# SwiGLU up projections with weight blocks stationary and high and low activations in one moving operand

## The chip, the cores and the metric

One core of one Trainium2 chip runs the whole program. The metric is the device time of one launch in microseconds, as the median of the runs shown.

## What is computed

Two layers work on 256 tokens of width 1024. Each layer is a feed-forward block, a mixer (projections, dilated and neighbourhood attention, gates, output projection) and a second feed-forward block, and a norm closes the program. The change is in the feed-forward blocks, whose inner width is 2816:

```python
def swiglu(x, w_up, w_down):
    gate, up = jnp.split(x @ w_up, 2, axis=-1)
    return (jax.nn.silu(gate) * up) @ w_down

for l in range(DEPTH):
    x = x + 0.5 * swiglu(rms_norm(x, ffn1_norm[l]), ffn1_w_up[l], ffn1_w_down[l])
    x = x + hybrid_mixer(rms_norm(x, mix_norm[l]), ...)
    x = x + 0.5 * swiglu(rms_norm(x, ffn2_norm[l]), ffn2_w_up[l], ffn2_w_down[l])
return rms_norm(x, final_norm)
```

## The kernel before

All large products run in split float32: each operand is a high part (rounded to fp32r) and a low part (the rest), and one product is three matmuls, high x high, high x low and low x high (`product`, L1017 to L1019). ScalarE (ACT) makes the high part of each weight unit (`hi`, L522), VectorE (DVE) the low part (`lo`, L721).

Weights come in units of 1 MB through a ring of three slots (`raw`, `w_hi`, `w_lo`). A unit's DMA is issued when the unit three before it has its low part; its high part is made when TensorE (PE) has finished with the unit three before (`split_free`). One feed-forward block is 33 units: 11 chunks of 256 hidden columns with three units each, two for the up projection (gate and up columns side by side, four of the eight k-blocks of 128 per unit) and one for the down projection.

In the up projection the normalised input's transpose (`a_hi`, `a_lo`, 128x128 blocks) is stationary and 512 weight columns move: 2 token halves x 8 k-blocks x 3 = 48 matmuls of 512 columns per chunk. ACT takes the tanh of the gate half (`tanh`, L575), DVE makes the gated tile `hidden` from it (`hide`, L800 and L803). PE turns `hidden` with four 128x128 transposes (`turn`, L1103), ACT and DVE split the turned tile (`hT_upper` L582, `hT_lower` L810), and the down product (24 matmuls of 512 columns) adds to four banks of 512 output columns, the groups g0 to g3. A chunk's down product runs one chunk late: PE's loop is first half of up(c), turn(c-1), second half of up(c), down(c-1). Each engine's queue is in the written order.

Between two blocks PE finishes the last down unit group by group; DVE adds each group to `x` (`update`, L732), PE transposes `x` (`input_transposes`, L1055), ACT and DVE split the result (`transposed_hi` L530, `transposed_lo` L745), ACT sums squares for the norm (L540) and GpSimd (POOL) turns the sums into `rstd`. The next block's first unit is split by `next_hi` and `next_lo` before those steps. In the mixer's output projection (units O_AT to O_AT+3) the groups end in the same way. In the first block, PE runs matmuls on a zero tile (`spin`, L1048) while the input arrives.

## Time and profile before

| | us |
|---|---|
| median of 3 runs (lowest, highest) | 1189.36 (1189.19, 1190.08) |
| the profiled execution | 1190.11 |
| its span | 1188.3 |
| granted TensorE clock, mean | 0.998 |

Busy time in the span: PE 1174.7 us (99%), PE's weight loads 965.4 us (81%), DVE 717.5 us (60%), ACT 561.7 us (47%), POOL 59.6 us (5%). Of the 5632 matmuls, 4560 belong to split products of 512 columns. Matmuls overlap each other in the profile, so that the step from one start to the next is the pace, and not the duration of one.

### The profile page before, as it was taken

The numbers are of one execution on the slowest core, as the hardware profiler recorded it, in microseconds if no ns is written. First come the engines' busy times: TensorE is split into PE (matmuls) and PEld (weight loads), VectorE is DVE, ScalarE is ACT, GpSimd is POOL, SyncE is SP. The second block draws the span as 40 slices with busy tenths as digits, with TensorE's granted clock in tenths as the row PEclk, the third lists the DMA queues.
The fourth block names the chain that finished last, engine by engine and source line by source line (L and its number), as shares of the span: only waits on it lengthen the run. The fifth ranks groups of instructions, "written<-read, shape, count | busy, mean of one in ns | idle before, by whom it ended". The sixth has DMA issues, their size and how long they took to land.

```text
span 1188.3 us, 15620 instructions
## 1 busy us (share of the span) xinstructions
PE 1174.7 (99%) x5632; PEld 965.4 (81%) x5632; DVE 717.5 (60%) x992; ACT 561.7 (47%) x767; POOL 59.6 (5%) x70
## 2 busy tenths in 40 slices
PE   8999999999999999999999999999999999999997
PEld 5888888888888888888888888878888888888885
DVE  4555556756766665555575555577557566655555
ACT  6444445555534544444464444465554445444342
POOL 3300003000200000000000000200002000000000
PEclk9999999999999999999999999999999999999999
DMA  9966555653434465555545555655443435655551
GB/s 269 288 208 205 181 204 176 206 177 109 141 130 154 152 211 186 194 178 199 187 164 193 182 187 195 230 177 177 142 142 107 164 138 177 213 191 197 179 174 36
DMA packets 145594, 211.47 MB, mean 178 GB/s; under 512 B 7648, under 2 KB 112272, under 8 KB 145296
## 3 DMA queue, kind: packets, MB, share of 16 engines
q1 hardware_dynamic: 142960, 206.33, 51.8%
q0 software_dynamic: 1920, 3.20, 1.2%
q10 hardware_dynamic: 672, 1.37, 0.4%
q8 instruction: 28, 0.46, 0.2%
q14 instruction: 14, 0.11, 0.0%
HBM read 209.77 MB, written 4.19 MB: 180 GB/s over the span
## 4 chain that ended last, share of the span: by engine, by line
PE 90%; DVE 4%; ACT 3%; issue 2%; DMA 0%; ACTq 0%; POOLq 0%; POOL 0%; DVEq 0%
PE bank L1017 28%; PE bank L1019 27%; PE bank L1018 27%; PE bank L1200 2%; PE bank L1173 2%; PE bank L1103 2%; DVE w_lo L721 1%; PE bank L1185 1%; ACT w_hi L522 1%; ACT a_hi L530 1%; DVE a_lo L745 1%; PE bank L1163 1%; ACT probs L540 1%; PE bank L1055 1%; DVE qk_raw L924 0%
## 5 line engine op out<-in xcount | busy, mean ns | idle before, releaser
L721 DVE TENSOR_TENSOR w_lo<-raw,w_hi 128x2048 fp32r<-128x2048 f32 x190 | 440.0, 2318 | 243.3 <-ACT w_hi L522 243.2
L522 ACT ACTIVATE w_hi<-raw 128x2048 fp32r<-128x2048 f32 x190 | 363.7, 1918 | 252.4 <-PE bank L1019 238.3
L1017 PE MATMUL bank<-w_hi,a_hi 128*128 128x512 f32 (+1 forms) x1152 | 460.5, 400 | 1.5 <-DVE probsT L803 0.4
L1019 PE MATMUL bank<-w_hi,a_lo 128*128 128x512 f32 (+1 forms) x1152 | 446.7, 388 | 0.0
L1018 PE MATMUL bank<-w_lo,a_hi 128*128 128x512 f32 (+1 forms) x1152 | 445.7, 387 | 0.0
L1017 PEld LDWEIGHTS bank<-w_hi,a_hi 128*128 128x128 f32 x1152 | 216.7, 188 | 49.5 <-issue 5.8
L1019 PEld LDWEIGHTS bank<-w_hi,a_lo 128*128 128x128 f32 x1152 | 216.4, 188 | 45.5
L1018 PEld LDWEIGHTS bank<-w_lo,a_hi 128*128 128x128 f32 x1152 | 217.0, 188 | 39.0
L1017 PE MATMUL bank<-w_hi,hT_hi 128*128 128x512 f32 x352 | 138.2, 393 | 0.4 <-DVE hT_lo L810 0.4
L1019 PE MATMUL bank<-w_hi,hT_lo 128*128 128x512 f32 x352 | 137.1, 389 | 0.0
L1018 PE MATMUL bank<-w_lo,hT_hi 128*128 128x512 f32 x352 | 137.0, 389 | 0.0
L582 ACT ACTIVATE hT_hi<-bank 128x256 fp32r<-128x256 f32 x88 | 29.5, 383 | 153.1 <-PE bank L1103 153.1
L575 ACT ACTIVATE probs<-bank,stat 128x256 f32<-128x256 f32 x88 | 41.8, 475 | 123.5 <-PE bank L1019 123.5
L1017 PEld LDWEIGHTS bank<-w_hi,hT_hi 128*128 128x128 f32 x352 | 66.1, 188 | 14.1 <-DVE w_lo L721 0.9
L1019 PEld LDWEIGHTS bank<-w_hi,hT_lo 128*128 128x128 f32 x352 | 66.1, 188 | 13.9
L1018 PEld LDWEIGHTS bank<-w_lo,hT_hi 128*128 128x128 f32 x352 | 66.1, 188 | 13.3
L810 DVE TENSOR_TENSOR hT_lo<-bank,hT_hi 128x256 fp32r<-128x256 f32 x88 | 33.6, 420 | 70.4 <-ACT hT_hi L582 70.3
L800 DVE SCALAR_TENSOR_TENSOR probs<-probs,bank 128x256 f32<-128x256 f32 x88 | 36.8, 419 | 30.4 <-ACT probs L575 30.4
L845 DVE COPY probsT<-bank 128x512 f32<-128x512 f32 (+1 forms) x40 | 23.4, 585 | 45.2 <-PE bank L1185 45.2
L641 ACT ACTIVATE probs<-probs,neg_top 128x256 f32<-128x256 f32 (+1 forms) x80 | 36.6, 460 | 23.9 <-DVE neg_top L871 23.9
L803 DVE SCALAR_TENSOR_TENSOR probsT<-probs,stat,bank 128x256 f32<-128x256 f32 x88 | 42.3, 481 | 3.1
L1200 PEld LDWEIGHTS bank<-v,probsT 128*128 128x128 f32 x256 | 34.7, 191 | 3.3
(89 smaller groups left out, 655.6 us busy)
## 6 DMA issues: line engine op xcount, KB each, us to landing
raw<-ffn_w_up_dram SPq DMA_DIRECT2D x172, 512.0 KB, 4.5
raw<-w_in_dram SPq DMA_DIRECT2D x92, 512.0 KB, 4.4
raw<-ffn_w_down_dram SPq DMA_DIRECT2D x88, 512.0 KB, 3.9
raw<-w_out_dram SPq DMA_DIRECT2D x16, 512.0 KB, 3.6
raw<-w_branch_b_dram SPq DMA_DIRECT2D x8, 512.0 KB, 3.8
bias_rows<-na_rel_bias_dram POOLq DMA_DIRECT2D x24, 128.0 KB, 6.1
...
```

The source lines that it names most:

```text
L522: act.activation(w_hi[slot][:, :], raw[slot][:, :], ACT.Copy).then_inc(hi_done, 1)
L575: act.activation(tanh_g[:, t, :], bank[UP[t]][:, 0:FC], ACT.Tanh, scale=half_rstd[:, t:t + 1]).then_inc(tanh_done, 1)
L582: act.activation(hT_hi[:, :, toks], bank[HT[t]][:, 0:2 * P].rearrange("p (k s) -> p k s", k=2), ACT.Copy).then_inc(hT_hi_done, 1)
L641: e = act.activation(part, part, ACT.Exp, bias=neg_top[:, h, t:t + 1], accum_out=den[:, h, t:t + 1])
L721: dve.tensor_tensor(w_lo[slot][:, :], raw[slot][:, :], w_hi[slot][:, :].bitcast(F32), ALU.subtract).then_inc(lo_done, 1)
L800: dve.scalar_tensor_tensor(gated[:, t, :], tanh_g[:, t, :], 1.0, bank[UP[t]][:, 0:FC], ALU.add, ALU.mult).then_inc(gated_done, 1)
L803: dve.scalar_tensor_tensor(hidden[:, t, :], gated[:, t, :], half_rstd2[:, t:t + 1], bank[UP[t]][:, FC:2 * FC], ALU.mult, ALU.mult).then_in ...
L810: dve.tensor_tensor(hT_lo[:, :, toks], bank[HT[t]][:, 0:2 * P].rearrange("p (k s) -> p k s", k=2), hT_hi[:, :, toks].bitcast(F32), ALU.sub ...
L1017: pe.matmul(dst, s_hi, m_hi, start=start, stop=False)
L1018: pe.matmul(dst, s_hi, m_lo, start=False, stop=False)
L1019: return pe.matmul(dst, s_lo, m_hi, start=False, stop=stop)
L1200: mm = pe.matmul(bank[OB][:, at:at + HD], probsT[:, hh, k - kts[0], t * P:(t + 1) * P], v[:, k, h * HD:(h + 1) * HD], start=k == kts[0], s ...
```

## The change

The up projection turns its operands round. `a_hi` and `a_lo` lie side by side in one tile `a_both`, 512 columns per k-block: 256 tokens high, 256 tokens low. The weight block of 128x128 is stationary. `w_hi` meets all 512 columns in one matmul (L1117, L1120); `w_lo` meets the 256 high columns (L1118). The result is [hidden column, token], in two banks for the gate half (`U_BANKS`) and two for the up half (`V_BANKS`). A unit is now one half of the up projection with all eight k-blocks. The gated tile comes out already transposed, so `turn` is gone.

ACT copies the low columns out of the banks (`u_lower`, `v_lower`), DVE adds the high ones (`u_half`, `v_half`), multiplies the gate half by the row of `half_rstd` and makes the gate and the product on tiles of 128x512; both split the result. Since the norm's factor is now along the free axis, PE turns it once per block (`turn_rows`, two transposes), and the up half's factor is applied in `update`, where `half_rstd` takes the place of 0.5. PE's loop is U(c), V(c), down(c-1).

At a block's end down(9) runs its first three groups, down(10) the first two, then follow the transposes of `x` and the remaining groups in turn; the mixer's last two units are interleaved alike. `input_begin`, `input_groups` and the first block's loads stand in another order.

PE, inside a chunk. Before, the middle of a chunk, with the turn between the two up units:

```order
L1017 MATMUL bank<-w_hi,a_hi 128x512
L1018 MATMUL bank<-w_lo,a_hi 128x512
L1019 MATMUL bank<-w_hi,a_lo 128x512
L1103 MATMUL bank<-cst,probsT 128x128 x4
L1017 MATMUL bank<-w_hi,a_hi 128x512
```

Now, from the first k-block of a half on (`a_both` holds both parts):

```order
L1117 MATMUL banks<-a_both,w_hi 128x512
L1118 MATMUL banks<-a_both,w_lo 128x256 x2
L1120 MATMUL banks<-a_both,w_hi 128x512
L1118 MATMUL banks<-a_both,w_lo 128x256
L1120 MATMUL banks<-a_both,w_hi 128x512
```

Three matmuls of 512 columns per k-block and token half became one of 512 and one of 256 per k-block and weight block, and no transpose is left.

DVE, from the end of the chunk loop to the next block. Before:

```order
L721 TENSOR_TENSOR w_lo<-raw,w_hi 128x2048 [waits hi_done]
L810 TENSOR_TENSOR hT_lo<-bank,hT_hi 128x2x128 [waits hT_hi_done] x2
L732 SCALAR_TENSOR_TENSOR x<-bank,x 128x512 [waits acc_done] x2
L745 SCALAR_TENSOR_TENSOR a_lo<-bank,gainT,a_hi 128x128 [waits xT_hi]
```

Now:

```order
L817 TENSOR_TENSOR gates<-banks,gates 128x512 [waits u_low_done]
L821 TENSOR_TENSOR gates<-gates,probsT 128x512 [waits u_read]
L745 TENSOR_TENSOR w_lo<-raw,w_hi 128x2048 [waits hi_done]
L827 SCALAR_TENSOR_TENSOR gates<-gates 128x512 [waits tanh_done]
L832 TENSOR_TENSOR gates<-banks,gates 128x512 [waits v_low_done]
L835 TENSOR_TENSOR probsT<-gates 128x512 [waits gated_done,v_read]
L839 TENSOR_TENSOR yT_lo<-probsT,yT_hi 128x512 [waits hT_hi_done]
L745 TENSOR_TENSOR w_lo<-raw,w_hi 128x2048 [waits hi_done]
L757 SCALAR_TENSOR_TENSOR x<-banks,stat,x 128x512 [waits acc_done] x2
L770 SCALAR_TENSOR_TENSOR a_both<-banks,gainT,a_both 128x128 [waits xT_hi]
```

The low part of the next block's first unit (the second L745) now stands behind the last gated tile's split, right before the updates of `x`.

PE, at the end of a feed-forward block, around the first transposes of `x`. Before:

```order
L1019 MATMUL bank<-w_hi,hT_lo 128x512
L1055 MATMUL bank<-cst,x 128x128 [waits x_updated]
L1055 MATMUL bank<-cst,x 128x128 x3
L1017 MATMUL bank<-w_hi,hT_hi 128x512
L1018 MATMUL bank<-w_lo,hT_hi 128x512
```

Now (`yT` holds the last chunk's gated tile, `hT` that of the chunk before):

```order
L1059 MATMUL banks<-w_hi,yT_lo 128x512
L1095 MATMUL banks<-cst,x 128x128 [waits x_updated]
L1095 MATMUL banks<-cst,x 128x128 x3
L1057 MATMUL banks<-w_hi,hT_hi 128x512
L1058 MATMUL banks<-w_lo,hT_hi 128x512
```

A group of down(9) now follows the transposes, where the third group of the last unit stood; one more group runs after the first transposes.

The core of the diff (of functions that are rewritten the added lines stand here, the removed ones are in the kernel above):

```diff
-        a_hi = sb("a_hi", [P, KT, SEQ], F32R)
-        a_lo = sb("a_lo", [P, KT, SEQ], F32R)
+        a_both = sb("a_both", [P, KT, 2, SEQ], F32R)
...
+        def blocks(flat, i):
+            return flat[:, i * NB:(i + 1) * NB].rearrange("p (b s) -> p b s", b=2)
+        u_low, u_sum, tanh_u, v_low = (blocks(flat_gates, 4 + i) for i in range(4))
+        flat_probsT = probsT[:, :, :, :].rearrange("p a t k -> p (a t k)")
+        hT, half_rstd_rows = blocks(flat_probsT, 0), flat_probsT[:, NB:NB + SEQ]
+        last_hT_hi, last_hT_lo = yT_hi[:, 0:2, :], yT_lo[:, 0:2, :]
...
+                    to = place[:, :].rearrange("p (k n) -> p k n", n=FC)
+                    for h in range(2):
+                        cols = src[:, :, 4 * h:4 * h + 4, a * D_FF:(a + 1) * D_FF]
+                        yield to[:, 4 * h:4 * h + 4, :], cols[l, :, :, bass.ts(c, FC)]
...
             load_x(sp, 0)
             first_part(0, 0)
             load_x(sp, 2)
+            first_part(1, 0)
+            load_x(sp, 3)
             first_part(0, 1)
...
             first_part(1, 1)
             for l in range(DEPTH):
...
+            def input_begin(l, ph, at):
+                sum_squares(ph, 0)
                 transposed_hi(ph, 0)
                 transposed_hi(ph, 1)
...
+                hi(l, at, 1)
+                sum_squares(ph, 1)
+                transposed_hi(ph, 2)
+                sum_squares(ph, 2)
+                transposed_hi(ph, 3)
+                sum_squares(ph, 3)
...
+                def u_lower(c):
+                    if isinstance(c, int) and c == 0:
+                        unit_used(act, l, at, 0)
+                    else:
+                        unit_used(act, l, at, -1, c)
+                    act.activation(u_low, U_BANKS[:, :, SEQ:2 * SEQ], ACT.Copy).then_inc(u_low_done, 1)
...
+                    act.wait_ge(u_scaled, ff * CHUNKS + c + 1)
+                    act.activation(tanh_u, u_sum, ACT.Tanh).then_inc(tanh_done, 1)
+                def hT_upper(c, dst):
+                    act.wait_ge(hT_done, ff * CHUNKS + c + 1)
+                    act.activation(dst, hT, ACT.Copy).then_inc(hT_hi_done, 1)
...
+                u_lower(CHUNKS - 1)
+                hi(l, at, F_UNITS - 1)
+                tanh(CHUNKS - 1)
+                v_lower(CHUNKS - 1)
+                hT_upper(CHUNKS - 1, last_hT_hi)
+                next_hi(l, f, at)
...
+                factor = 0.5 if (ph - 1) % PHASES == 1 else half_rstd[:, t:t + 1]
...
+                transposed_lo(ph, 2)
+                transposed_lo(ph, 3)
...
+                def u_half(c):
+                    n = ff * CHUNKS + c + 1
+                    dve.wait_ge(u_low_done, n)
+                    dve.tensor_tensor(u_sum, U_BANKS[:, :, 0:SEQ], u_low, ALU.add).then_inc(u_read, 1)
+                    dve.wait_ge(u_read, n)
+                    if isinstance(c, int) and c == 0:
+                        dve.wait_ge(rows_ready, ff + 1)
+                    dve.tensor_tensor(u_sum, u_sum, half_rstd_rows.unsqueeze(1).to_broadcast([P, 2, SEQ]),
+                                      ALU.mult).then_inc(u_scaled, 1)
+                def gate(c):
+                    n = ff * CHUNKS + c + 1
+                    dve.wait_ge(tanh_done, n)
+                    dve.scalar_tensor_tensor(tanh_u, tanh_u, 1.0, u_sum, ALU.add, ALU.mult).then_inc(gated_done, 1)
+                def v_half(c):
+                    n = ff * CHUNKS + c + 1
+                    dve.wait_ge(v_low_done, n)
+                    dve.tensor_tensor(v_low, V_BANKS[:, :, 0:SEQ], v_low, ALU.add).then_inc(v_read, 1)
+                    dve.wait_ge(v_read, n)
+                    dve.wait_ge(gated_done, n)
+                    dve.tensor_tensor(hT, tanh_u, v_low, ALU.mult).then_inc(hT_done, 1)
+                def hT_lower(c, dst, upper):
+                    dve.wait_ge(hT_hi_done, ff * CHUNKS + c + 1)
+                    dve.tensor_tensor(dst, hT, upper.bitcast(F32), ALU.subtract).then_inc(hT_lo_done, 1)
+                lo(l, at, 2)
+                u_half(0)
+                gate(0)
+                v_half(0)
+                lo(l, at, 3)
+                lo(l, at, 4)
+                hT_lower(0, hT_lo[:, :, :], hT_hi[:, :, :])
+                with dve.Fori(1, CHUNKS - 1) as c:
+                    u_half(c)
                     lo(l, at, 2, c)
...
+                    gate(c)
+                    v_half(c)
+                    lo(l, at, 3, c)
+                    lo(l, at, 4, c)
+                    hT_lower(c, hT_lo[:, :, :], hT_hi[:, :, :])
+                u_half(CHUNKS - 1)
+                lo(l, at, F_UNITS - 1)
+                gate(CHUNKS - 1)
+                v_half(CHUNKS - 1)
+                hT_lower(CHUNKS - 1, last_hT_lo, last_hT_hi)
                 next_lo(l, f, at)
...
             def rope(l, i):
...
+            def up(slot, pair, ks):
+                for b in range(2):
+                    for k in ks:
+                        at = k * FC + b * P
+                        w = w_hi[slot][:, at:at + P]
+                        both = a_both[:, k, :, :].rearrange("p h s -> p (h s)")
+                        if k == 0:
+                            mm = pe.matmul(pair[:, b, :], w, both, start=True, stop=False)
+                        mm = pe.matmul(pair[:, b, 0:SEQ], w_lo[slot][:, at:at + P], a_hi[:, k, :], start=False, stop=False)
+                        if k > 0:
+                            mm = pe.matmul(pair[:, b, :], w, both, start=False, stop=k == KT - 1)
+                return mm
+            FIRST, SECOND = range(0, KT // 2), range(KT // 2, KT)
+            def turn_rows(l, ph):
+                pe.wait_ge(rstd_ready, ph + 1)
+                for t in range(TT):
+                    tr = pe.transpose(bank[ROWS][:, t * P:(t + 1) * P], half_rstd[:, t:t + 1].to_broadcast([P, P]), ident)
+                tr.then_inc(rows_turned, 1)
+            def first_products(l, ph, at):
+                if ph == 0:
+                    input_transposes(0, 1)
                     spin(5)
...
+                    pe.wait_ge(part_lo, 1)
+                    pe.wait_ge(xT_lo, 2)
+                    up(0, U_BANKS, FIRST)
+                    input_transposes(0, 2)
+                    input_transposes(0, 3)
+                    pe.wait_ge(part_lo, 2)
+                else:
+                    split_ready(l, at, 0)
+                    pe.wait_ge(xT_lo, ph * 4 + 2)
+                    input_transposes(ph, 2)
+                    up(0, U_BANKS, FIRST)
+                    input_transposes(ph, 3)
+                    split_ready(l, at, 1)
+                up(1, V_BANKS, FIRST)
+                split_ready(l, at, 0)
+                pe.wait_ge(xT_lo, ph * 4 + 4)
+                up(0, U_BANKS, SECOND).then_inc(split_free, 1)
+                turn_rows(l, ph)
+                split_ready(l, at, 1)
+                up(1, V_BANKS, SECOND).then_inc(split_free, 1)
...
+                def down(c, slot, s_hi, s_lo, start):
+                    pe.wait_ge(hT_lo_done, done + c + 1)
+                    for g, (t, n) in enumerate(GROUP4):
+                        mm = rows(slot, s_hi, s_lo, 0, t, n, bank[ACC[t][n]], start, False)
+                    mm.then_inc(split_free, 1)
+                def up_pair(c):
                     split_ready(l, at, -1, c)
...
+                    pe.wait_ge(u_read, done + c)
+                    up(2, U_BANKS, range(KT)).then_inc(split_free, 1)
                     split_ready(l, at, 0, c)
...
+                    pe.wait_ge(v_read, done + c)
+                    up(0, V_BANKS, range(KT)).then_inc(split_free, 1)
+                first_products(l, ph, at)
+                def chunk(c, first):
+                    up_pair(c)
                     split_ready(l, at, 1, c)
...
+                    down(c - 1, 1, hT_hi, hT_lo, first)
+                chunk(1, True)
                 with pe.Fori(2, CHUNKS - 1) as c:
...
+                    chunk(c, False)
+                up_pair(CHUNKS - 1)
+                order = groups(ph + 1)
+                def group(slot, s_hi, s_lo, g, stop):
+                    t, n = order[g]
+                    return rows(slot, s_hi, s_lo, 0, t, n, bank[ACC[t][n]], False, stop)
+                split_ready(l, at, F_UNITS - 2)
+                pe.wait_ge(hT_lo_done, done + CHUNKS - 1)
+                for g in range(3):
+                    group(1, hT_hi, hT_lo, g, False)
                 split_ready(l, at, F_UNITS - 1)
...
+                pe.wait_ge(hT_lo_done, done + CHUNKS)
+                for g in range(2):
+                    group(2, last_hT_hi, last_hT_lo, g, True).then_inc(acc_done, 1)
+                next_transposes(ph + 1, 0)
+                group(1, hT_hi, hT_lo, 3, False).then_inc(split_free, 1)
+                next_transposes(ph + 1, 1)
+                group(2, last_hT_hi, last_hT_lo, 2, True).then_inc(acc_done, 1)
+                group(2, last_hT_hi, last_hT_lo, 3, True).then_inc(split_free, 1)
             def next_transposes(ph, g):
...
+                split_ready(l, M_AT, O_AT + 2)
+                pe.wait_ge(mT_lo, l * 4 + 4)
+                for g in range(3):
+                    group(2, g, False, False)
+                split_ready(l, M_AT, O_AT + 3)
+                for g in range(2):
+                    group(3, g, False, True).then_inc(acc_done, 1)
+                input_transposes(ph + 1, 0)
+                group(2, 3, False, False).then_inc(split_free, 1)
+                input_transposes(ph + 1, 1)
+                group(3, 2, False, True).then_inc(acc_done, 1)
+                group(3, 3, False, True).then_inc(split_free, 1)
```

## Rows read from the trace of the kernel before

**Rows 1.** The page, part 1: busy time, share of the span, instructions.

```profile
PE 1174.7 (99%) x5632; PEld 965.4 (81%) x5632; DVE 717.5 (60%) x992; ACT 561.7 (47%) x767; POOL 59.6 (5%) x70
```

**Rows 2.** Timeline of PE at two turns: start, length (us), line, operands, count.

```profile
99.35 0.60 PE L1103 MATMUL bank<-cst,probsT 128*128 128x128 f32 x4
...
115.24 0.39 PE L1019 MATMUL bank<-w_hi,a_lo 128*128 128x512 f32 x1
...
115.92 0.39 PE L1019 MATMUL bank<-w_hi,a_lo 128*128 128x512 f32 x1
116.15 0.60 PE L1103 MATMUL bank<-cst,probsT 128*128 128x128 f32 x4
...
116.82 0.39 PE L1018 MATMUL bank<-w_lo,a_hi 128*128 128x512 f32 x1
```

**Rows 3.** Timeline of PE and its weight loads where 256 columns move.

```profile
252.06 0.28 PE L1018 MATMUL bank<-w_lo,a_hi 128*128 128x256 f32 x1
252.06 0.19 PEld L1019 LDWEIGHTS bank<-w_hi,a_lo 128*128 128x128 f32 x1
252.18 0.28 PE L1019 MATMUL bank<-w_hi,a_lo 128*128 128x256 f32 x1
```

**Rows 4.** Groups by line and shape: count, busy us, mean ns, idle before.

```profile
L721 DVE TENSOR_TENSOR w_lo<-raw,w_hi 128x2048 fp32r<-128x2048 f32 x190 | 440.0, 2318 | 243.3 <-ACT w_hi L522 243.2
...
L522 ACT ACTIVATE w_hi<-raw 128x2048 fp32r<-128x2048 f32 x190 | 363.7, 1918 | 252.4 <-PE bank L1019 238.3 <-DMA raw<-ffn_w_up_dram 12.5 <-DMA raw<-ffn_w_down_dram 1.3
...
L833 DVE TENSOR_TENSOR gates<-qk_raw,cst 128x512 f32<-128x512 f32 x24 | 15.0, 686 | 0.0
...
L672 ACT ACTIVATE a_hi<-bank 128x512 fp32r<-128x512 f32 x8 | 4.6, 598 | 19.2 <-PE bank L1220 19.2
```

**Rows 5.** Timeline, end of the first feed-forward block and start of the mixer.

```profile
192.76 2.29 DVE L721 TENSOR_TENSOR w_lo<-raw,w_hi 128x2048 fp32r<-128x2048 f32 x1
...
195.52 0.47 PE L1017 MATMUL bank<-w_hi,hT_hi 128*128 128x512 f32 x1 [0.23 <-DVE hT_lo L810]
...
198.37 0.60 PE L1055 MATMUL bank<-cst,x 128*128 128x128 f32 x4
...
199.01 1.14 ACT L530 ACTIVATE a_hi<-bank,gainT 128x128 fp32r<-128x128 f32 x4 [1.48 <-PE bank L1055]
...
211.18 0.39 PE L1019 MATMUL bank<-w_hi,a_lo 128*128 128x512 f32 x1
211.71 0.50 PE L1017 MATMUL bank<-w_hi,a_hi 128*128 128x512 f32 x1
```

**Rows 6.** Timeline of the first 27 us, PE, DVE, ACT and POOL.

```profile
7.68 1.11 PE L1055 MATMUL bank<-cst,x 128*128 128x128 f32 x4 [1.57 <-DMA x<-x_dram]
8.59 2.34 PE L1048 MATMUL bank<-warm 128*128 128x512 bf16 x5
...
14.03 1.24 PE L1048 MATMUL bank<-warm 128*128 128x512 bf16 x5
...
10.95 1.12 DVE L745 SCALAR_TENSOR_TENSOR a_lo<-bank,gainT,a_hi 128x128 fp32r<-128x128 f32 x4
...
19.51 0.21 ACT L540 ACTIVATION_READ_ACCUMULATOR probs<-x 128x1 f32 x1
...
21.47 0.20 POOL L464 TENSOR_TENSOR stat<-stat 128x2 f32<-128x2 f32 x1
...
26.60 0.47 PE L1017 MATMUL bank<-w_hi,a_hi 128*128 128x512 f32 x1 [0.41 <-DVE probsT L803]
```

**Rows 7.** Timeline of the last matmuls and the end on DVE.

```profile
1179.04 0.39 PE L1019 MATMUL bank<-w_hi,hT_lo 128*128 128x512 f32 x1
...
1176.79 0.68 DVE L732 SCALAR_TENSOR_TENSOR x<-bank,x 128x512 f32<-128x512 f32 x1
...
1179.09 0.75 DVE L773 TENSOR_SCALAR gates<-gates,stat 128x1024 f32<-128x1024 f32 x1 [0.66 <-POOL stat L502]
...
1181.09 0.68 DVE L732 SCALAR_TENSOR_TENSOR x<-bank,x 128x512 f32<-128x512 f32 x1
```

217 lines of the change are left out of this document (56 added, 161 removed).

## The prediction

> **What bounds the kernel now.** I read the page's busy shares first: PE is busy 99% of the span, DVE 60%, ACT 47% [rows 1]. Busy matmuls overlap, so this alone proves nothing; the timeline must show that one starts as soon as the one before lets it. Three 512-column matmuls take 0.68 us from start to start (115.24 to 115.92), 0.2267 us each, through whole chunks [rows 2]. DVE and ACT wait for PE or for each other: ACT's `hi` idles 252.4 us in all, nearly all of it for PE [rows 4]. So every matmul taken away shortens the span by its step, unless PE then waits; the other engines matter only where one of their chains ends later than PE's cover. Such places are the block boundaries, the start and the end.
>
> **Inside a chunk.** One chunk lasts from the turn at 99.35 to the turn at 116.15, 16.79 us unrounded [rows 2]. Its 72 products of 512 columns are 72 x 0.2267 = 16.32. The turn therefore costs 0.47: four transposes, and slightly wider steps behind them (115.92 to 116.82 holds the turn and one product). It goes 44 times: **-20.7 us**.
>
> The up products move the same number of columns: before 48 x 512 = 24,576 per chunk, now 32 x 512 + 32 x 256 = 24,576. But there are 64 matmuls in place of 48. Where 256 columns move before, the step is 0.12 us (252.06 to 252.18), with a weight load of 128 columns beside each [rows 3]. Half of 0.2267 is 0.113: a matmul has a fixed part of about 0.013. Now a chunk's up products take 32 x (0.2267 + 0.120) = 11.09 against 48 x 0.2267 = 10.88, +0.21. I count 43 chunks, since the first one is in the start below: **+9.2**. The row turns of `half_rstd` are two transposes of about 0.11 each in three blocks (the first again in the start): **+0.65**.
>
> That fixed part decides half of the gain. The Trainium skill, page "TensorE: Matmul & The Clock Gate", section "Back-to-back issue gap", gives N/2.4 + 2.5 ns for a warm matmul. By it the 16 added matmuls would cost 0.04 us a chunk and the whole change would come out 7 us better than by my sum. The trace does not agree for these products (0.2267 and 0.120 are 13 ns over the columns' time), and I keep the trace.
>
> **Does the new vector work stay covered?** Per chunk ACT makes three `hi` (1.92 each) and four steps of 512 columns (about 0.6 each, as L672), 8.2 us; DVE three `lo` (2.32) and six steps of 0.69 (as L833), 11.1 us [rows 4]. Both are below the new chunk of 11.09 + 24 x 0.2267 = 16.53. In order, with U(c) starting at 0: U's banks are read by 6.9 and needed at 16.5; V's are read by 12.5 and needed at 22.1; the low part of down(c) is ready at 20.8 and its `hT_lo` at 21.4, needed at 27.6. At least 6 us of cover each, so zero. Without it a late step would cost PE its lateness 44 times.
>
> **At the end of a feed-forward block.** Let V(10) end at 0. PE has down(9) g0 to g2 (18 x 0.2267 = 4.1), then down(10) g0 and g1, to 6.8. The new chain is `v_lower`, add, multiply, `hT_upper`, `hT_lower`: 0.2 + 0.6 + 0.7 + 0.7 + 0.65 + 0.7 with hand-overs, 3.65; covered by 0.4. But ACT makes the next unit's `hi` only after `hT_upper` (2.85 to 4.77) and DVE its `lo` only after `hT_lower`, 4.8 to 7.1. Queued behind it is the first `update`, whose group was ready at 5.65. It ends at 7.7, and the transposes of `x`, with PE free at 6.8, wait 0.95. Before, that `lo` ran earlier, under the last down products (192.76) [rows 5]. Three of the four blocks have a successor: +2.85. What goes in exchange is the wait for the last turned tile in each layer's first feed-forward (195.52: the row shows 0.23 as idle, and with the slow refill behind the turn I take 0.39): two times, -0.8.
>
> **At the start of a block.** Transposes reach ACT 0.64 after they start (198.37 to 199.01), four splits are 1.14 on ACT [rows 5] and 1.12 on DVE [rows 6]. Before, PE has a hole of 0.53 - 0.23 = 0.30 in front of the last token half's products (211.18 to 211.71) [rows 5], and some 0.17 ahead of it, at all five boundaries: -2.3. Afterwards the first feed-forward product needs both token halves, since all 256 tokens move at once. DVE splits g0, does the third `update`, then splits g1: ready 0.62 after PE is. Three blocks: +1.9. In the mixer the third unit's `hi` now stands behind all splits and squares; by the same steps its low part comes 0.7 late, while the old hole closes: two times, +1.4. Boundaries together: 2.85 - 0.8 - 2.3 + 1.9 + 1.4 = **+3.0**.
>
> **Start.** Now the first product needs the second token half's `lo`, at 12.07 [rows 6]. Eight pairs of 512 and 256 columns are 2.77 us at 2.4 GHz. The third and fourth transposes of `x` stand behind them, and behind those the splits, the `hi` and `lo` of half a unit (estimated at 1.07 and 1.23, a little over half of the rows for 2048 columns [rows 4]) that the second half of U needs, four squares of about 0.61, and POOL's five steps: 1.95 from the last square (19.72) to their end at 21.67 [rows 6]. The turn of the row waits for those. V(0) then ends at 27.75, where before U(1) began at 26.60 [rows 6]; and V(1) waits 0.3 for its low part. That is +1.45.
>
> The clock adds to it. Five warm matmuls at 8.59 take 2.34 us, five at 14.03 only 1.24 [rows 6]: PE was at the 1.2 GHz level and rose to 2.4 after unbroken work from 7.68 on. The changed PE has nothing between 10.7 and 12.1. If the rise comes as early as before (about 13.5), +1.45 stands. If it comes after as long a run as before, at about 17 to 18, the first eight pairs take 5.1 us, part of V is covered, and everything behind is 1.65 later. I take the late rise, as the hole breaks the run: **+3.1**. The Trainium skill, same page, section "What's actually happening", says that "the default state is throttled, and activity releases the throttle", which fits both rows; it doesn't say which of the two I shall see.
>
> **End.** Before, the last product ends at about 1179.27, but DVE starts the last `update` only at 1181.09, because the first half's scaling (1179.09) stands ahead [rows 7]. Afterwards groups g0 and g1 end one group (1.36) earlier against the last, so the chain g0, g1, scaling, g2 fits: the last `update` starts 0.4 after the last product in place of 1.8. **-1.4**.
>
> **Sum.** -20.7 + 9.2 + 0.65 + 3.0 + 3.1 - 1.4 = -6.15. Against the profiled execution, a span of 1188.3 in 1190.11, that is 1182.2 in 1184.0; this execution is 0.75 above the median shown. **Forecast 1183.2 us.** A difference under 0.2% (2.4 us) can't be told from none with this kernel.
>
> **Rivals.**
> (a) The boundaries hide the next unit's split after all and the clock rises as early as before: -3.0 - 1.65 more, 1178.6. For it: my chains are built of single steps, and neighbours in the queues overlap by up to 0.1 each. Against: the `lo` of 2.3 us really stands ahead of the `update` in DVE's order. 0.20, with what lies between.
> (b) Changing the moving width costs what it costs beside transposes, about 3.5 ns (115.92 to 116.15 is 0.23 [rows 2]). With 1408 changes: +4.9, 1188.1, no change to be seen. Rows 3 have equal widths only, so nothing excludes it. 0.13.
> (c) The chain behind U and V in a block's first chunk runs late, as `lo` of the next units and the gate share DVE in fixed order: about 1 us more in each of four blocks, some 1187; I count half of it as faster. 0.12.
> (d) Slower: a 256-column product doesn't cover its weight load. A load shows 0.19 us, its product's step 0.12 [rows 3]; if two loads could not overlap across different widths, each short product would take 0.19: 1408 x 0.068 = +96, about 1279. It decides from 0.126 us per short product on, where the time passes 1191.8. The Trainium skill, same page, section "The mechanism" of its part 3, says that weight loads overlap running matmuls only when the row groups differ. By that the 16 added loads would stand bare; rows 3 show full-height loads starting with the running matmul. 0.05.
> (e) The change doesn't remove what it says: excluded by the instruction order, which has no turn left.
>
> **How the numbers follow.** Forecast 0.50; (a) 0.20; (b) 0.13; (c) 0.12; (d) 0.05. Faster by over 0.2% (under 1187.0): forecast, (a) and half of (c), 0.76; within 0.2%: (b) and the rest of (c), 0.19; slower 0.05. The range reaches from (a) to (b), 1178.5 to 1188.3; it leaves out (d) and the tails.
>
> **What the new profile would show.** Chunk period 16.53 to 16.6 between equal places of the loop; steps of 0.227 and 0.120 in alternation; PE idle 0.95 before the first transposes of `x` behind three feed-forward blocks, with DVE's `w_lo` as the releaser's queue neighbour; 0.6 before the first product of a block; U(1) starting at 29 (late clock) or 27.7 (early); last product to last `update` about 0.4. I am wrong if the short products step at 0.124 or more, if PE idles inside the loop, or if the boundaries' sum is outside 0 to 6 us.

## The result, and the profile after

The changed kernel takes 1197.84 us (median of six runs, 1194.55 to 1199.79), the kernel before 1189.16 (1188.57 to 1190.08). The ratio is 1.0069, with a 95% interval of 1.0049 to 1.009: slower by about 0.7%, where I had forecast 0.5% faster. The profiled execution took 1194.55, with a span of 1192.7; my sum gave a span of 1182.2. The 10.5 us between these two are what the rest of the text looks for.

Busy time of the kernel after, the page's part 1:

```profile
PE 1165.4 (98%) x6158; PEld 979.9 (82%) x6158; DVE 791.6 (66%) x992; ACT 589.6 (49%) x771; POOL 59.5 (5%) x70
```

Against [rows 1] PE has 9 us less work, and yet the span is 4.4 us longer: PE now waits. To see where, I took the time between the first transposes of `x` of successive blocks (us; the two last columns are kernels of the experiments):

| from, to | before | after | two_fixes | best_last_only |
|---|---|---|---|---|
| start, end of layer 0's first feed-forward | 198.37 | 202.23 | 198.39 | 196.69 |
| mixer 0 | 207.83 | 207.89 | 207.87 | 206.55 |
| layer 0's second feed-forward | 187.33 | 186.62 | 186.61 | 186.89 |
| layer 1's first feed-forward | 187.80 | 190.43 | 187.41 | 186.37 |
| mixer 1 | 207.87 | 207.93 | 207.92 | 206.58 |
| layer 1's second feed-forward and end | 199.10 | 197.58 | 197.63 | 197.48 |

(In after and two_fixes the transposes stand one group, 1.36 us, earlier in the work than in before, which shortens the first row and lengthens the last; in best_last_only only those behind the mixers do.) The two feed-forwards that stand ahead of a mixer are the slow ones. Nothing in the change treats them otherwise than the other two.

**The chunk.** PE of the kernel after, the same place of the loop one chunk apart, and the steps inside (start, length):

```profile
467.00 0.39 PE L1117 MATMUL banks<-a_both,w_hi 128*128 128x512 f32 x1
...
483.63 0.39 PE L1117 MATMUL banks<-a_both,w_hi 128*128 128x512 f32 x1
...
484.33 0.28 PE L1118 MATMUL banks<-a_both,w_lo 128*128 128x256 f32 x1
484.44 0.40 PE L1120 MATMUL banks<-a_both,w_hi 128*128 128x512 f32 x1
484.69 0.28 PE L1118 MATMUL banks<-a_both,w_lo 128*128 128x256 f32 x1
484.81 0.40 PE L1120 MATMUL banks<-a_both,w_hi 128*128 128x512 f32 x1
485.04 0.28 PE L1118 MATMUL banks<-a_both,w_lo 128*128 128x256 f32 x1
```

A chunk lasts 16.63 us (16.627 unrounded), not 16.53. From 484.33 to 485.04 are two pairs in 0.71; over many pairs the mean is 0.350, where I had 0.2267 + 0.120 = 0.347, which over the 32 pairs of a chunk makes the 0.1. The short product goes in 0.112 to 0.120, as forecast; the wide one takes 0.234 in the mean. The down products still step 0.2267.

**The mask add.** Near the end of both slow blocks POOL adds the mask to the bias tile of the coming mixer, and DVE's `hT_lo` starts while it runs. Kernel after, POOL, DVE and PE (in brackets the idle time before, and who ended it):

```profile
182.91 7.35 POOL L492 TENSOR_TENSOR bias<-bias,cst 128x3072 f32<-128x3072 f32 x1 [130.14 <-DMA bias<-bias_rows]
...
183.47 7.34 DVE L839 TENSOR_TENSOR hT_lo<-probsT,hT_hi 128x512 fp32r<-128x512 f32 x1
...
190.96 0.47 PE L1057 MATMUL banks<-w_hi,hT_hi 128*128 128x512 f32 x1 [0.49 <-DVE hT_lo L839]
...
197.80 0.47 PE L1057 MATMUL banks<-w_hi,yT_hi 128*128 128x512 f32 x1 [2.49 <-DVE yT_lo L839]
```

`hT_lo` takes 7.34 us; elsewhere 0.69. It ends at 190.81, which is the end of POOL's add (190.26) plus 0.55: it stood still until POOL was done. Everything behind it in DVE's queue is then late, and PE waits twice. The same four rows stand at 768 to 783 (7.33 on DVE, waits of 0.49 and 2.51). (The brackets count idle time from the modelled end of the matmul before. Where the text gives 0.65 or 2.65 for such a wait, it counts from when the next start was due, one step behind the last one; that is 0.16 more.) The same add ran in the kernel before:

```profile
181.29 7.70 POOL L482 TENSOR_TENSOR bias<-bias,cst 128x3072 f32<-128x3072 f32 x1 [130.66 <-DMA bias<-bias_rows]
...
184.16 0.76 DVE L810 TENSOR_TENSOR hT_lo<-bank,hT_hi 128x256 fp32r<-128x256 f32 x2 [1.84 <-ACT hT_hi L582]
186.24 4.91 DVE L721 TENSOR_TENSOR w_lo<-raw,w_hi 128x2048 fp32r<-128x2048 f32 x1 [1.33 <-ACT w_hi L522]
```

There it held `w_lo` (4.91 in place of 2.3, its end 2.16 behind POOL's). That cost PE little (the 0.23 of [rows 5] is the wait behind it). `hT_lo` of the kernel before read a PSUM bank and one tile of SBUF, and none of its 88 instances was held (0.414 to 0.426 us), though two of them ran inside this very add (184.16), and two in layer 1's. The change gave it two SBUF inputs. The Trainium skill, page "SBUF — State Buffer", section "SBUF: two separate sides", says that a DVE operation with two SBUF inputs and a POOL operation that reads SBUF share a pair of ports, by "an **exclusive lock**, not a bandwidth split". The rows agree, to half a microsecond.

The longer wait costs twice. Columns: window and length, busy time of each engine, then the granted clock, the DMA share and GB/s:

```profile
190.00:198.00 8.00, 5.02 (x22) 3.67 (x21) 6.89 (x8) 2.81 (x4) 0.26 (x1) 1.00 0.31 95
198.60:202.00 3.40, 3.40 (x10) 2.63 (x9) 2.95 (x2) 0.38 (x2) 0.00 (x0) 0.51 0.08 25
203.00:210.00 7.00, 7.00 (x35) 5.71 (x34) 5.22 (x12) 4.57 (x11) 0.00 (x0) 1.00 0.36 127
```

Behind the wait the clock is at the 1.2 GHz level from 198.6 to 202.0, which costs 1.7 us. At the second place, behind a wait as long, it stayed at 2.4. The three other traced kernels with these waits (after_again, spread_late, widths_grouped) show the same: 3.4 us at half clock at the first place, none at the second. Why the places differ isn't shown.

**The start.** Kernel after, SP, POOL, ACT and PE:

```profile
23.38 4.22 POOL L486 DMA_DIRECT2D bias_rows<-na_rel_bias_dram  x5
...
25.79 0.98 SPq L331 DMA_DIRECT2D raw<-ffn_w_up_dram  x2
...
26.58 0.40 PE L1117 MATMUL banks<-a_both,w_hi 128*128 128x512 f32 x1
...
41.67 1.92 ACT L532 ACTIVATE w_hi<-raw 128x2048 fp32r<-128x2048 f32 x1 [8.70 <-DMA raw<-ffn_w_up_dram]
...
45.97 0.50 PE L1117 MATMUL banks<-a_both,w_hi 128*128 128x512 f32 x1 [2.38 <-DVE w_lo L745]
```

The weights of U(2) are asked for at 25.79 in two transfers of 512 KB, and the second one arrives 15.9 us later, 15.3 after its own issue, where the page gives 4.2 for the median one. In between POOL's queue issues the first 15 of the 24 copies that spread the bias table. The kernel before had the same copies, and its transfer was slow as well (issued at 24.02, 11.6 us), but PE did not wait for it. U(1) starts at 26.58: in this execution the clock had come up at 10.9, before the first product and earlier than in either branch of my forecast.

**The turns and the end.** DVE and PE around the second block boundary, the third unit of the mixer, and the last product with the last `update`:

```profile
593.74 2.29 DVE L745 TENSOR_TENSOR w_lo<-raw,w_hi 128x2048 fp32r<-128x2048 f32 x1 [1.11 <-ACT w_hi L532]
595.94 1.40 DVE L757 SCALAR_TENSOR_TENSOR x<-banks,stat,x 128x512 f32<-128x512 f32 x2
...
596.75 0.66 PE L1095 MATMUL banks<-cst,x 128*128 128x128 f32 x4 [0.80 <-DVE x L757]
602.54 0.63 PE L1095 MATMUL banks<-cst,x 128*128 128x128 f32 x4 [0.56 <-issue]
...
219.76 0.50 PE L1057 MATMUL banks<-w_hi,a_both 128*128 128x512 f32 x1 [0.48 <-DVE w_lo L745]
...
1184.61 0.39 PE L1059 MATMUL banks<-w_hi,yT_lo 128*128 128x512 f32 x1
...
1185.48 0.74 DVE L757 SCALAR_TENSOR_TENSOR x<-banks,stat,x 128x512 f32<-128x512 f32 x1
```

These are the waits that I had forecast, nearly to size (see below).

### The profile page after: what moved, and what is told of

Its sections match the earlier page's. It is cut to its first block, busy times and chain, and to the rows that moved or that the text cites. A ratio compares the mean times of both kernels' runs of the same rounds, so it can differ in the third digit from the quotient of the medians.

```text
span 1192.7 us, 16475 instructions
## 1 busy us (share of the span) xinstructions
PE 1165.4 (98%) x6158; PEld 979.9 (82%) x6158; DVE 791.6 (66%) x992; ACT 589.6 (49%) x771; POOL 59.5 (5%) x70
## 4 chain that ended last, share of the span: by engine, by line
PE 89%; DVE 5%; ACT 2%; DMA 1%; issue 1%; POOLq 0%; POOL 0%; SPq 0%; ACTq 0%; DVEq 0%
PE banks L1120 22%; PE banks L1057 15%; PE banks L1059 15%; PE banks L1058 15%; PE banks L1118 13%; PE banks L1117 3%; PE banks L1264 2%; DVE w_lo L745 2%; PE banks L1237 2%; DMA raw<-ffn_w_up_dram 1%; ACT w_hi L532 1%; DVE hT_lo L839 1%; PE banks L1249 1%; PE banks L1095 1%; PE banks L1227 1%
## 5 line engine op out<-in xcount | busy, mean ns | idle before, releaser
L745 DVE TENSOR_TENSOR w_lo<-raw,w_hi 128x2048 fp32r<-128x2048 f32 x190 | 434.3, 2290 | 188.4 <-ACT w_hi L532 188.2
L1120 PE MATMUL banks<-a_both,w_hi 128*128 128x512 f32 x1232 | 439.4, 396 | 0.0
L1118 PE MATMUL banks<-a_both,w_lo 128*128 128x256 f32 x1408 | 364.4, 279 | 1.3 <-DVE w_lo L1032 1.3
L1118 PEld LDWEIGHTS banks<-a_both,w_lo 128*128 128x128 f32 x1408 | 265.4, 188 | 16.5 <-DVE w_lo L1032 1.6
L1120 PEld LDWEIGHTS banks<-a_both,w_hi 128*128 128x128 f32 x1232 | 231.2, 188 | 47.2
L1057 PE MATMUL banks<-w_hi,a_both 128*128 128x512 f32 (+1 forms) x448 | 181.6, 405 | 1.3 <-DVE w_lo L745 1.0
L1059 PE MATMUL banks<-w_hi,a_both 128*128 128x512 f32 (+1 forms) x448 | 172.1, 384 | 0.0
L1058 PE MATMUL banks<-w_lo,a_both 128*128 128x512 f32 (+1 forms) x448 | 171.5, 383 | 0.0
L1057 PE MATMUL banks<-w_hi,hT_hi 128*128 128x512 f32 x320 | 125.1, 391 | 1.0 <-DVE hT_lo L839 1.0
L1059 PE MATMUL banks<-w_hi,hT_lo 128*128 128x512 f32 x320 | 124.5, 389 | 0.0
L1058 PE MATMUL banks<-w_lo,hT_hi 128*128 128x512 f32 x320 | 124.5, 389 | 0.0
L1057 PEld LDWEIGHTS banks<-w_hi,a_both 128*128 128x128 f32 x448 | 84.4, 188 | 20.7 <-issue 4.0
L1059 PEld LDWEIGHTS banks<-w_hi,a_both 128*128 128x128 f32 x448 | 84.2, 188 | 17.5
L1117 PE MATMUL banks<-a_both,w_hi 128*128 128x512 f32 x176 | 70.2, 399 | 3.6 <-DVE w_lo L745 2.4
```

The source lines that it names most:

```text
L745: dve.tensor_tensor(w_lo[slot][:, :], raw[slot][:, :], w_hi[slot][:, :].bitcast(F32), ALU.subtract).then_inc(lo_done, 1)
L1057: pe.matmul(dst, s_hi, m_hi, start=start, stop=False)
L1058: pe.matmul(dst, s_hi, m_lo, start=False, stop=False)
L1059: return pe.matmul(dst, s_lo, m_hi, start=False, stop=stop)
L1117: mm = pe.matmul(pair[:, b, :], w, both, start=True, stop=False)
L1118: mm = pe.matmul(pair[:, b, 0:SEQ], w_lo[slot][:, at:at + P], a_hi[:, k, :], start=False, stop=False)
```

## The experiments

All are compared with the kernel before on the same chip, whose median lay between 1188.9 and 1189.5 us each time. My theory after reading the traces: POOL's lock costs some 6 us and the late weights some 2 to 5; the rest is the wide product's step. The rivals: the width switching of rival (b), and the new order at the turns.

**after_again**, the changed kernel once more.

> The changed kernel once more, to have it on the chip of the runs beside it and to see whether the 5 us between its runs (1194.6 and 1199.8) follow TensorE's clock. Clock theory: one chunk loop period is 16.63 in every execution, and runs near 1199 show additional stretches at half clock behind waits of TensorE, each worth 1.7 us per 3.4 us. Chip theory (the chip or the DMA differ, not the clock): the same number of half-clock stretches, and a longer wait at the start for the weights.

Measured: 1196.45 us, ratio 1.0057 [1.0039, 1.0076]. Its profile has the waits at the same places (0.66 and 2.66 ahead of both mixers, 1.7 for the weights). The question of the 5 us between runs stays open: these runs lie between 1195.5 and 1198.5, and no execution near 1199 was profiled. What the traces show is that the wait for the weights varies, 1.7, 2.5, 3.8 and 4.1 us in the four that have it, and that behind the two longest the clock is at 1.2 GHz for 3.4 us.

**bias_by_head**: the mask add in eight pieces, so that the lock is let go between them.

```diff
-                pool.tensor_tensor(rows, rows, na_mask..., ALU.add).then_inc(bias_ready, 1)
+                for h in range(NA_HEADS):
+                    part = pool.tensor_tensor(bias[:, h, :, :], bias[:, h, :, :], na_mask..., ALU.add)
+                part.then_inc(bias_ready, 1)
```

> GpSimd adds the mask to the bias tile in eight instructions of about 1 us, one for each head, in place of one of 7.4 to 8 us at the end of the first feed-forward of each layer. Lock theory (a VectorE instruction with two inputs in SBUF waits until a running GpSimd instruction that reads SBUF is through): the hT_lo split that took 7.34 us at 183.47 takes at most about 1.7, TensorE's waits of 0.67 and 2.65 us behind it go in both layers, so 6.6 us less, and 1.6 to 3.4 us more where the clock fell behind the wait. Rival (the chain of vector steps is too long by itself at a block's end, or the weights come late there because the 1.5 MB bias transfer runs): the waits stay, less than 1 us gained.

Measured: 1191.85 us, ratio 1.0019 [1.0, 1.0039], 4.6 less than after_again, where I had expected 6.6 or more. Its runs spread over 7.9 us, and its profile has the longest of the waits for the weights (4.06 at 49.73, with a half clock behind it). `hT_lo` is held for one piece only:

```profile
187.46 4.68 POOL L492 TENSOR_TENSOR bias<-bias,cst 128x384 f32<-128x384 f32 x3 [133.53 <-DMA bias<-bias_rows]
...
188.77 1.51 DVE L840 TENSOR_TENSOR hT_lo<-probsT,hT_hi 128x512 fp32r<-128x512 f32 x1
190.83 0.69 DVE L818 TENSOR_TENSOR gates<-banks,gates 128x512 f32<-128x512 f32 x1 [0.55 <-ACT gates L582]
...
192.64 3.08 DVE L746 TENSOR_TENSOR w_lo<-raw,w_hi 128x2048 fp32r<-128x2048 f32 x1
...
187.46 13.39 POOL L492 TENSOR_TENSOR bias<-bias,cst 128x384 f32<-128x384 f32 x8 [133.53 <-DMA bias<-bias_rows]
```

(The last row is from a view of POOL alone.) The rows show two things more. The step at 190.83 reads one PSUM bank and one tile of SBUF and is not held. And the hold works both ways: the eight pieces take 13.39 us in place of 7.35, since POOL now waits for DVE's steps as well; the piece beside the `w_lo` of 3.08 lasts 3.06, and the one beside the PSUM read at 190.83 takes 1.02.

Layer 1's first feed-forward falls from 190.43 to 187.45, so the lock costs 3.0 us there. At the first place the waits are as long (0.49 and 2.49), and the clock costs 1.7 more.

**spread_late**: the bias copies wait until the first four chunks' gate sums are made.

```diff
             norm_factors(0)
+            pool.wait_ge(u_scaled, 4)
```

> GpSimd issues its 24 bias_rows transfers only after the fourth chunk of the first block (about 80 us) in place of from 23.4 us on. Queue theory (these transfers hold up the weight transfer issued at 25.8, which lands at 41.7): the weights land some 5 us after issue, TensorE's wait of 2.54 us at 45.97 goes, 2.5 us less; in the later chunks 6 us of cover hide the same delay. Rival (the wait comes from the order of the first loads: the third unit's slot is freed 1.8 us later than before): the wait stays about the same.

Measured: 1194.15 us (1192.67 to 1194.93), ratio 1.0031 [1.0015, 1.0048], 2.3 less. The wait for the weights is gone, and in two_fixes, which has this edit too, the same transfer takes 6.3 us (28.08 to 34.38): so the copies were what kept the weights back. By which resource isn't shown. The spread of the runs is smaller with it (2.3 us, against 2.9 and 5.2 of the changed kernel).

**widths_grouped**: of each weight block's products those of 256 columns together, then those of 512 (the first one of a bank stays ahead of them). The edit in short:

```diff
+                    for k in ks: (w_lo block k, 256 columns)
+                    for k in ks: (w_hi block k, 512 columns)
```

> In the up products of each weight block the 256-column matmuls of all k run together and then the 512-column ones, in place of alternating. Switching theory (the pair of 512 and 256 columns takes 0.350 us against 0.347 for the sum of equal ones, for each change of width): the chunk period falls from 16.63 to about 16.54, 44 x 0.09 = 4 us less. Rival (512 columns read from the tile with both parts take 0.233 in themselves, in whatever order): the period stays within 0.02 of 16.63.

Measured: 1195.4 us, ratio 1.005 [1.0036, 1.0064]; chunk period 16.613 against 16.627. With a seventh of the width changes (8 a chunk in place of 56) the period gives back 0.6 us of some 4; the median is 1.05 below after_again, less than the spread of the runs. Rival (b) as I had put it, a price per change, falls. (It also counted 32 changes a chunk, where the order has 56.)

**two_fixes**: bias_by_head and spread_late together.

> Both at once: the mask added head by head, and the bias_rows transfers issued only from the fourth chunk on. Additive theory: without the GpSimd waits (6.6 us), the half clock behind them (1.7) and the weight wait at the start (1.7 to 4.1, in some executions with another 1.7 at half clock), some 11 us less than the changed kernel beside it: about 1186, that is 2 to 4 us faster than before, and runs within 1 us of each other if the spread came from the weight wait. Rival (a common limit, say the weight transfers, so that the second fix finds nothing left): about 1191.

Measured: 1187.7 us, ratio 0.9986 [0.9977, 0.9996]. That is 8.75 below after_again (on another chip), and 4.5 above my forecast. I had expected 1186. Part of what is missing is a wait that the late products had hidden: the first transposes of `x` at 198.39 now wait 1.1 us for the `update`. Another 0.44 at each place (194.45) is left of the lock, behind a `yT_lo` that the held steps made late.

**before_by_head**: the kernel before with the add in pieces, to see what the lock cost there.

> The kernel before with the mask added head by head. Lock theory: its w_lo step of 4.91 us at 186.24 takes 2.3 to 3.3, the wait of 0.39 us at 195.5 and 778.5 goes, 0.8 us less in all: the kernel before had the same lock, but under cover. Rival (the 0.39 come from the turned tile's own chain): no change in them.

Measured: 1188.13 us, ratio 0.9992 [0.9983, 1.0002]. The two first feed-forwards are 0.6 and 0.5 shorter, and PE's wait at 195.5 is gone; the median is 1.3 less, and the interval allows up to 2. So the lock did cost the kernel before something near 1 us, and most of the gain of bias_by_head belongs to the change.

**two_spin9**: two_fixes with nine warm-up products in place of five ahead of the first product.

> As two_fixes, with nine warm matmuls in place of five while the second token half is split. Clock theory (the hole of 1.4 us before the first product leaves TensorE at half clock for the first products): the first products run at full clock, and the second block of products starts about 1.7 us earlier. Rival (the clock falls or rises whatever stands in that hole, by work further back): no difference, or a loss of up to 0.4 us where nine matmuls at half clock end later than the split.

Measured: 1187.13 us, ratio 0.9978 [0.9968, 0.9987]; 0.6 less, inside the two intervals' overlap. The profile still has a half clock from 13.0 to 16.4.

**two_lo_later**: two_fixes with the split of the next block's first unit behind DVE's second `update`.

```diff
                 update(l, ph, at, 0)
                 update(l, ph, at, 1)
+                (the lo that next_lo made ahead of them)
```

> As two_fixes, and the low part of the next block's first unit made behind the second update of x, not ahead of the first. Queue theory (that step of 2.3 us stands in front of the update for which TensorE's transposes wait): the waits of 1.1 and 0.96 us before the first transposes of x behind a feed-forward block go in three places, and of that wait about 0.3 comes back before the first products of the block behind the second feed-forward: 2.5 to 3 us less than two_fixes. Rival (the first update is late anyway, or what is gained is lost at the next step): less than 1 us.

Measured: 1184.49 us, ratio 0.9957 [0.9941, 0.9974], 3.2 less than two_fixes. That is my term "next unit's split ahead of the update" (2.85), removed.

**two_plain_end**: two_fixes with down(9) whole ahead of down(10), as before the change.

```diff
-                for g in range(3): group(1, ...)
+                for g in range(4): group(1, ...)
...
-                group(1, hT_hi, hT_lo, 3, False).then_inc(split_free, 1)
-                next_transposes(ph + 1, 1)
                 group(2, last_hT_hi, last_hT_lo, 2, True).then_inc(acc_done, 1)
+                next_transposes(ph + 1, 1)
```

> The changed kernel with the mask add by head and the bias copies held back, and with the last two down units of every feed-forward block in plain order: all four groups of the ninth, then the four of the tenth. This undoes the part of the change that interleaves them. My ledger priced that part at 1.4 us gained at the program's end (the last update starts one group, 1.36 us, earlier in relation to the others) and some cover for the two turns of the next block's x. So I expect 1187.7 + 1.4 = 1189.1 us, with the next x transposes one group later in the work. The rival is that the interleaving only shifts when the turns are asked for, and brings waits of its own since the ninth unit's slot comes free later: then the plain order is as fast or faster, 1186.5 to 1187.7.

Measured: 1185.78 us, ratio 0.9967 [0.9954, 0.998]. A miss: I had expected 1.4 more, and it is 1.9 less. The rows of the first turn, two_fixes and then two_plain_end:

```profile
198.39 0.66 PE L1096 MATMUL banks<-cst,x 128*128 128x128 f32 x4 [0.94 <-DVE x L758]
```

```profile
198.28 0.66 PE L1096 MATMUL banks<-cst,x 128*128 128x128 f32 x4 [0.17 <-DVE x L758]
```

DVE's updates start at 197.6 in one and 197.5 in the other. The interleaving brings the transposes forward by a group of PE's work, but not what they wait for. At the turns it costs 1.5, 1.0 and 0.8 us (intervals, corrected by 1.36); at the end of the program it gains 1.3, as forecast.

**best_last_only**: two_fixes with the plain order in the first three feed-forwards and the interleaved one in the last, with the grouping and nine warm-up products.

> The changed kernel with the mask add by head, the bias copies held back, the 256-column products of a block grouped and nine warm-up products, and with the last two down units interleaved in the last block alone, in plain order in the three others. If interleaving costs at the turns (0.8 to 1.5 us each by the trace, 3.3 in all) and pays 1.3 at the end, this takes both: 1185.8 of the plain order, - 1.3 for the end, - 0.6 for the grouping = 1183.9 us. If the plain order had been faster for another reason, its end among them, it stays 1185.2 or more.

Measured: 1182.33 us (1181.86 to 1183.26), ratio 0.9939 [0.9921, 0.9957]. The best version, 0.6% faster than the kernel before. It is 1.6 below my 1183.9, and the profiled execution gains as much in the first row of the table alone (198.28 in two_plain_end, 196.69 here), where the clock came up at 12.0, ahead of the first product. Whether the nine warm-up products do that isn't settled: in two_spin9 they did not.

**all_spin9** has the other remedy, the later split, with interleaving everywhere, and the grouping and the nine warm-up products too.

> The changed kernel with the POOL mask add by head, the bias copies held back until the first weights are in, each block's 256-column products grouped, the split of the next block's first weight unit moved behind the second update of x, and nine warm-up products at the start in place of five. Each piece had a price when it ran alone or beside the first two: grouping takes 0.014 us off each of 43 chunk periods (0.6 us), moving the split 3 us, the warm-up nothing that a span showed. If the pieces do not share anything they add: 1184.5 - 0.6 = about 1183.9 us, ratio to the kernel before 0.995. If the start gains from the warm-up after all (full clock at the first product in place of the half clock for 3.4 us, up to 1.7 us), 1182.2. If grouping only paid where waits stood that the fixes have taken away: 1184.5.

Measured: 1182.56 us, ratio 0.9944 [0.993, 0.9957], level with it; its profile has the full clock at the first product as well. **best_last_lo** has both remedies.

> best_last_only with the split of the next block's first weight unit moved behind the second update of x as well. If both edits take away the same wait (the transposes of x wait for an update that stands behind this split on VectorE), it gives nothing more: 1182.3 us, give or take 0.5. If they are two costs, up to 3 us less: 1179.5 us.

Measured: 1184.3 us, ratio 0.9963 [0.9949, 0.9977]. They take away the same wait, and together they make a new one: the third transposes now wait for splits of `a_both`, ahead of which DVE makes the moved `w_lo` (591.67 to 593.95). The row of best_last_lo (the same wait is 1.05 in best_last_only):

```profile
596.78 0.63 PE L1099 MATMUL banks<-cst,x 128*128 128x128 f32 x4 [2.15 <-DVE a_both L771]
```

**The wide step.** Five kernels on why 512 columns of `a_both` take 0.234 us beside 256-column products. **two_probe** and **two_probe2** run such products, and other pairs of operands, behind the last down product.

> Behind the last down product the kernel runs six rows of 32 products with 512 moving columns, whose results nobody reads (about 45 us more than the version without them). In order: weight block stationary and [high|low] activations moving, as the changed up projection has them; weight block stationary and weights moving; activations stationary and [high|low] moving; activations stationary and weights moving, as the kernel before has them; the first again with two PSUM banks in turn; the first again with one block and one moving operand 32 times. In the kernel the first form steps 0.231 to 0.233 us and the last form of the kernel before 0.227. If the moving tile is the reason (its address or how it lies), rows 1, 3, 5 and 6 step 0.231 and rows 2 and 4 0.227. If the stationary operand is (weight blocks read from a wide tile), rows 1, 2, 5 and 6 step 0.231, 3 and 4 0.227. If it is the company of the up projection, its other waits and other engines' reads of the same tile, all six step 0.227, as nothing else runs by then.

> Behind the last down product four rows of 32 products with 512 moving columns, results unread (30 us more). Row 1 pairs weight block (b, k) with the activations of the same k, as the up projection does; row 2 the same blocks with the activations of k = 0 and 4 alone; row 3 the blocks of k = 0 and 4 with the activations of each k; row 4 block k with the activations of k + 4. If two addresses that are read at once (the next weight load and the running stream) are the reason, row 1 shows steps that depend on k, mean near 0.231 us as in the loop, and the rows with other pairs show other patterns or 0.227 throughout. If other engines' traffic in the loop is the reason, all four rows step 0.227.

Measured: all ten rows step 0.2267 (means 0.2266 to 0.2267), so neither operand nor their pairing is slow by itself. **two_pad1024** and **two_pad128** move `a_both`, and all tiles behind it, in memory.

```diff
+        sb("pad", [P, 1024 // 4])
         a_both = sb("a_both", [P, KT, 2, SEQ], F32R)
```

> An unused tile of 1024 bytes a partition stands ahead of the activation tile, so that it and all tiles behind it lie 1024 bytes higher. If the distance between weight blocks and moving activations in memory is the reason for the 0.231 us step, it changes here: to 0.227 (chunk period 16.53 us, 4 us off the program, 1184 us) or to a larger one. If traffic of other engines is the reason, the step stays 0.231 to 0.233, the period 16.63 and the time near 1187.7 us.

> The same with 128 bytes. Under the address theory the pattern of the steps over k moves or goes, period between 16.53 and 16.7 us; under the traffic theory it stays 16.63 us and the time near 1187.7 us.

Measured: 1187.3 and 1198.31 us, one run each. 1024 bytes change nothing (period 16.626). 128 bytes make each chunk 0.167 longer, in two_pad128's rows:

```profile
484.07 0.40 PE L1119 MATMUL banks<-a_both,w_hi 128*128 128x512 f32 x1
...
500.87 0.40 PE L1119 MATMUL banks<-a_both,w_hi 128*128 128x512 f32 x1
```

The down products, of which only the stationary operand moved, go from 0.2269 to 0.2324 there. An address matters, then, but it is not what makes the wide step of the kernel as it stands. **two_probe3** has the short products in the quiet, and each of the other engines' work beside wide ones alone.

> Behind the last down product: 48 products of 512 moving columns in the quiet; then four times eight pairs of a 256-column and a 512-column product, as the up projection has them; then four times eight 256-column products with eight of 512 behind; then three rows of 48 of 512 columns, the first with a weight transfer of 1 MB running, the second with ScalarE's 128x2048 copies, the third with VectorE's 128x2048 subtractions. About 66 us more than the version without; results unread. If the 256-column products are the reason (a backlog of weight loads that the next wide product pays), the pairs take 0.350 us and the 512s of the grouped rows 0.229 to 0.230 in the mean with the first ones slowest, in the quiet, and the last three rows step 0.227. If the other engines' traffic is the reason, the pairs take 0.347 or less and one of the last three rows steps 0.231 or more: the transfers' if the pattern over k is fixed by addresses, ScalarE's or VectorE's if it is the shared memory ports.

Measured, in order: pairs of 256 and 512, groups of eight, then wide ones beside a transfer, ScalarE's copies and VectorE's subtractions.

```profile
1188.96 0.40 PE L1422 MATMUL banks<-a_both,w_hi 128*128 128x512 f32 x1
...
1190.02 0.40 PE L1422 MATMUL banks<-a_both,w_hi 128*128 128x512 f32 x1
```

```profile
1200.63 0.64 PE L1426 MATMUL banks<-a_both,w_lo 128*128 128x256 f32 x4
1201.10 2.00 PE L1422 MATMUL banks<-a_both,w_hi 128*128 128x512 f32 x8
1202.94 0.52 PE L1426 MATMUL banks<-a_both,w_lo 128*128 128x256 f32 x3
```

```profile
1211.78 3.56 PE L1422 MATMUL banks<-a_both,w_hi 128*128 128x512 f32 x15
```

```profile
1221.75 5.60 PE L1422 MATMUL banks<-a_both,w_hi 128*128 128x512 f32 x24
```

```profile
1232.63 7.64 PE L1422 MATMUL banks<-a_both,w_hi 128*128 128x512 f32 x33
```

Three pairs take 1.06, 0.353 each, with no other engine at work. Eight wide products behind eight short ones take 1.84, 0.230 each; single steps are 0.233, 0.236, 0.228, 0.232, 0.231 and then 0.227. Beside a transfer, ACT or DVE wide products alone take (5.60 - 0.39) / 23 = 0.2265 and the like. So it is the short products, and not traffic: they leave something behind that the next wide products pay. The kernel before shows it too, behind the four narrow transposes of its turn. These are its steps from 100.03 on: 0.231, 0.236, 0.228, 0.233, 0.231 and then 0.226, nearly the series above.

```profile
100.03 0.39 PE L1018 MATMUL bank<-w_lo,a_hi 128*128 128x512 f32 x1
100.26 0.40 PE L1019 MATMUL bank<-w_hi,a_lo 128*128 128x512 f32 x1
100.49 0.39 PE L1017 MATMUL bank<-w_hi,a_hi 128*128 128x512 f32 x1
```

That it is a backlog of weight loads (0.19 each, beside steps of 0.12) is my reading; no run shows it.

## Why the prediction was wrong

By its own steps, for the profiled execution (span 1182.2 forecast, 1192.7 measured):

- **"At least 6 us of cover each, so zero."** This step failed, and it is the largest: 3.0 us at each of two places and 1.7 of clock, +7.7. In exchange the wait for the update, 1.1 us in two_fixes at 198.39, does not show at the first turn, where everything is late already: +6.6 in all. The cover was right for steps of 0.69. One of them took 7.34, since the change gave it a second SBUF input while POOL's mask add ran. The kernel before showed such a hold, and I had not looked at what POOL did: with 5% busy it seemed no party. A sign of it stood in my own sum: the 0.39 us at 195.52 that I booked to the turned tile (the term of -0.8) were the lock's, for they are gone in before_by_head. I took a mean duration, 2.32 [rows 4], without asking for the longest. The view of one line has it; `w_lo` in the kernel before, shortest, median and longest in ns:

```profile
L721 DVE TENSOR_TENSOR w_lo<-raw,w_hi x190: 2281/2293/4909, 21.6 to 1164.9; 128x2048 fp32r<-128x2048 f32 x190
```

- **The fixed part of the up products.** What failed is the term 32 x (0.2267 + 0.120): it lets a wide product cost 0.2267 whatever stands before it, and behind a short one it costs 0.234. I took 0.347 for a pair from rows in which all products had 256 columns or all had 512. Measured 0.350: 16.627 against 16.53, times 43, +4.2. The 0.120 of [rows 3] held for the short product. What I had called "slightly wider steps" behind the turn looks like the same price in the kernel before, and I did not carry it over to wide products behind short ones. The Trainium skill, page "TensorE: Matmul & The Clock Gate", section "Back-to-back issue gap", gives N/2.4 + 2.5 ns for an isolated product; by it a pair would take an estimated 0.325, and the trace does not agree. Rival (b) had nearly the size (4.9), and its mechanism, a price per change of width, fell with widths_grouped.
- **The start.** Here the sum held a wrong branch and missed a wait. I forecast U(1) at 29 with the late clock; it was at 26.58 here (-2.4), with a clock that came up before the first product, which neither branch had, and at 28.84 in two_fixes, where the clock came up at 17.1, as the late branch says. What I had left out is the transfer: +2.5 here. The change issues the weights 1.8 us later and POOL's copies run beside them, as they did before. That the two come out even is luck: in two_fixes, with the late clock and no such wait, the late branch stands.
- Together 6.6 + 4.2 + 0.1 = 10.9, against 10.5 to explain. The 0.4 between them lies in the small boundary terms, which I can't split that finely.
- **The boundaries** were right, but for the first turn. Wait for the update behind the split: 0.95 forecast, 0.96 at 596.74 and 1.17 at 787.17. First product of a block: 0.62 forecast, 0.66 to 0.72. Third unit of the mixer: 0.7 forecast, 0.64 and 0.65. But I booked the interleaving as a gain at the end (1.4; 1.3 measured) and did not see that the 0.95 was its own price: in the plain order the wait is 0.17.
- **The turns.** -20.7 could not be told apart from the added products; their sum per chunk is -0.166 where I had -0.263.

two_fixes, in which the first and third failure are removed, comes to 1187.7, 4.5 over the forecast of 1183.2; the mis-sized pair explains 4.2 of it. The gate chain, rival (c), is not late: from the first product on PE shows no wait in the first chunk of the second, third and fourth feed-forward. Nor does (d) hold: a short product costs 0.12.
